# Decay functions and scans of a head, moved between the masks of the head before it

## The chip, the core and the metric

The kernel runs on one core of a Trainium2 chip. The metric is the device time of one execution in microseconds (us); lower is better. The five engines of a core are named as the profile names them: PE (TensorE; PEld is its weight load), DVE (VectorE), ACT (ScalarE), POOL (GpSimd) and SP (SyncE, which issues the DMAs here). Each works through its own instructions in order; they wait for each other by semaphores.

## The reference

One step of a diffusion trunk of two layers for 512 latent and 128 context tokens of width 1024. Layer 0 mixes tokens with HGRN2 (8 heads), layer 1 with GLA (4 heads); each layer ends with a PEER channel mixer, in which most of the time is spent. The change touches the two mixers only. Per head and direction they compute:

```python
# HGRN2: the decay of a head, per direction
f = lb_d + (1.0 - lb_d) * jax.nn.sigmoid(f_pre)
log_f = jnp.log(jnp.maximum(f, F_MIN))
k = (1.0 - lb_d) * jax.nn.sigmoid(-f_pre)
# GLA: the decay of a head, per direction
log_g = jax.nn.log_sigmoid(gk) / GATE_NORM
# both: a chunk of the scan, forward and on reversed tokens
bcum = jnp.cumsum(gi, axis=2)
o_inter = einsum('bhtd,bhde->bhte', qi * jnp.exp(bcum), S)
decay = where(causal, jnp.exp(jnp.minimum(diff, 0.0)), 0.0)
att = einsum('bhtd,bhtsd,bhsd->bhts', qi, decay, ki)
o = o_inter + einsum('bhts,bhse->bhte', att, vi)
S = exp(b_last) * S + einsum('bhsd,bhse->bhde', ki * exp(b_last - bcum), vi)
```

GLA's q, k and v also pass a 3 by 3 depthwise convolution and a silu first.

## The kernel before

`mixer` (line 445) runs both kinds of mixer, one head after the other: `head(h, final)` of each engine stands in a loop over all heads but the last, and once more for the last. Tokens are the 640 columns of every tile, channels the 128 partitions. The order of the work is written out by hand, engine by engine; nothing schedules it.

**Projections.** A head's inputs come from the weight in chunks of 128 columns: HGRN2 has five (v, og, then the early ones ff, fb, q), GLA six (v0, v1, og0, og1, then k, q) and two small gate products. The early chunks of head h + 1 are projected during head h. For each chunk SP loads it (`w_raw`), ACT rounds it (`hi`, line 659, `w_hi`), POOL forms the remainder (`lo`, line 621, `w_lo`), and PE multiplies three times per part (line 440), in two halves of 320 columns with a PSUM bank `pp` each; a half's bank is free for the next chunk once ACT has copied it out (line 679). ACT splits a chunk's weight right behind the copy that frees the buffer (`next_hi`).

**A head, HGRN2.** ACT takes two sigmoids of the gate inputs and one of q (lines 730 to 734). DVE makes the gates of them (856 to 864), ACT takes the logarithm (738), DVE corrects it (870) and scans it, forward and backward, into `b2` (814, 815), which releases POOL by `b_ready`. DVE forms the differences to the chunk's end (876), ACT exponentiates `b2` and them into `e2` and `t2` (742, 743), DVE multiplies q and k in (884, 885) and PE transposes the result and v (975). Then states are formed (984, 901). The seven levels of the in-chunk decay (`exponents`, 556 to 559) are differences, three levels on POOL, four on DVE; ACT exponentiates them (757), DVE weights them with q and k (906, 910) and counts `weighted`. Meanwhile PE projects the early chunks of the next head.

**The mask loop.** For each of five token tiles t, PE computes the scores (996, 997), DVE applies the masks (916, `am`), PE multiplies with v and the states (1013), ACT copies the output (762, `oT`). PE runs the scores of one tile ahead of the products. After the fifth tile the next head begins with its sigmoids on ACT, while PE starts to project its v.

**GLA** differs thus: ACT makes the decay by Abs, Exp and Ln (707 to 711), DVE finishes and scans it (834, 837, 814, 815). In the mask loop DVE has the convolutions of the next head's k and q (794, 803, 805); those of v follow in the head, once v0 and v1 are copied; `silu` (829) and ACT's sigmoid (717) follow each.

POOL's order in a head is: the remainders of chunks 2 and 3, the differences of three levels, the remaining remainders, chunks 0 and 1 of the next head last.

Of the kernel before, what the change touches and what calls it, by code (L numbers as in the profile page):

```python
# [11 lines left out]
ALU = mybir.AluOpType  # L12
ACT = mybir.ActivationFunctionType
# [12 lines left out]
F_MIN = 1e-20  # L26
# [418 lines left out]
def mixer(nc, a, c, mx, h_hi, h_lo, oT, og_sp, out, layer):  # L445
# [15 lines left out]
    with ExitStack() as s:  # L461
# [155 lines left out]
        def _(pool):  # L617
# [6 lines left out]
            def head(h, final):  # L624
                for j in range(2, min(4, NCH)):
                    if j < L or not final:
                        lo(h, j)
                pool.wait_ge(b_ready, h + 1)
                for l in range(POOL_LEVELS):
                    exponents(pool.tensor_tensor, l)  # L630
                    pool.drain().then_inc(pool_diff, 1)
                if not final:
                    for j in range(4, NCH):
                        lo(h, j)
                    lo(h + 1, 0)
                    lo(h + 1, 1)
# [16 lines left out]
        def _(act):  # L653
# [41 lines left out]

            def output_gates(h, n, final):
                if n == 0:
                    act.wait_ge(og_out, h * 16 + 16)
                copy(og[:, n, :], NV + n, h)
                next_hi(h, NV + n, final)  # L700

            def head(h, final):

                if mx.gla:

                    act.drain()
                    act.activation(b2[:, :, :], g2[:, :, :], ACT.Abs)
                    act.drain()
                    act.activation(b2[:, :, :], b2[:, :, :], ACT.Exp, scale=-1.0)
                    act.drain()  # L710
                    act.activation(b2[:, :, :], b2[:, :, :], ACT.Ln, bias=c["one"][:, 0:1])
                    act.drain().then_inc(ln_done, 1)
# [15 lines left out]
                else:  # L728
                    act.drain()
                    act.activation(k2[:, :, :], g2[:, :, :], ACT.Sigmoid, scale=-1.0)  # L730
                    act.drain()
                    act.activation(g2[:, :, :], g2[:, :, :], ACT.Sigmoid)
                    act.drain().then_inc(sig_done, 1)
                    act.activation(zc[:, 1, :], zc[:, 0, :], ACT.Sigmoid).then_inc(q_sig_done, 1)
                    copy(v[:, 0, :], 0, h)
                    next_hi(h, 0, final)
                    act.wait_ge(f_ready, h + 1)
                    act.activation(t2[:, :, :], t2[:, :, :], ACT.Ln).then_inc(ln_done, 1)
# [12 lines left out]
                for n, levels in ((1, (0, 1, 2)), (2, (3, 4, 5, 6)), (3, ())):  # L751
# [6 lines left out]
                    if n < E + mx.extra and not final:  # L758
                        early(h, n)
                for t in range(NT):  # L760
                    act.wait_ge(o_done, h * NT + (1 + t + 1))
                    act.activation(oT[:, bass.ds(h * NV, NV), t * P:(t + 1) * P],
                                   pO[:, 0:NV, :], ACT.Copy).then_inc(o_out, 1)

# [9 lines left out]
            for n in range(E + mx.extra):  # L774
                early(-1, n)
            with act.Fori(0, H - 1) as h:
                head(h, False)
# [3 lines left out]
        def _(dve):  # L781
# [42 lines left out]
            dve.sem_inc(masked, 1)  # L824
            def head(h, final):
                if mx.gla:
                    def silu(j):
# [5 lines left out]
                    dve.wait_ge(ln_done, h + 1)  # L833
                    nc.vector.scalar_tensor_tensor(g2[:, :, :], g2[:, :, :], 0.0, b2[:, :, :],
                                                   ALU.min, ALU.subtract)
                    dve.drain()
                    nc.vector.tensor_scalar(g2[:, :, :], g2[:, :, :], 1.0 / 16.0, None, ALU.mult)
                    dve.drain()
                    scan(h)
# [11 lines left out]
                else:  # L851

                    dve.wait_ge(sig_done, h + 1)
                    for d in range(2):
                        oml = c["oml"][:, bass.ds(h + 8 * d, 1)]
                        nc.vector.tensor_scalar(t2[:, d, :], g2[:, d, :], oml, c["lb"][:, bass.ds(h + 8 * d, 1)],
                                                ALU.mult, ALU.add)
                        nc.vector.tensor_scalar(k2[:, d, :], k2[:, d, :], oml, None, ALU.mult)
                    dve.drain()
                    nc.vector.tensor_scalar(t2[:, :, :], t2[:, :, :], F_MIN, None, ALU.max)  # L860
                    dve.drain()
                    nc.vector.tensor_scalar(g2[:, :, :], t2[:, :, :], LN_LOW, LN_UP, ALU.is_lt, ALU.mult)
                    dve.drain()
                    nc.vector.scalar_tensor_tensor(t2[:, :, :], g2[:, :, :], 1.0, t2[:, :, :], ALU.add, ALU.mult)
                    dve.drain().then_inc(f_ready, 1)
# [3 lines left out]
                    dve.wait_ge(ln_done, h + 1)  # L869
                    nc.vector.scalar_tensor_tensor(g2[:, :, :], g2[:, :, :], LN_FIX, t2[:, :, :], ALU.mult, ALU.add)  # L870
                    dve.drain()
                    scan(h)
# [39 lines left out]
                for t in range(NT):  # L912
# [5 lines left out]
                    if mx.gla and not final and t < 4:  # L918

                        dve.wait_ge(copied, halves_done(h, L + t // 2, 1))  # L920
                        conv(h + 1, t // 2, t % 2)

            if mx.gla:
                for j in range(2):
                    dve.wait_ge(copied, halves_done(-1, L + j, 1))
                    conv(0, j, 0)
                    conv(0, j, 1)
            with dve.Fori(0, H - 1) as h:
                head(h, False)
# [3 lines left out]
        def _(pe):  # L933
# [90 lines left out]
            head(H - 1, True)  # L1024

# [995 lines left out]
```

## Time and profile before

| | |
|---|---|
| median of 3 runs | 5023.19 us (5022.8 to 5024.14) |
| the profiled execution | 5024.39 us, its span 5022.6 us |
| busy, share of the span | PE 84%, PEld 75%, DVE 75%, POOL 38%, ACT 32% |
| a head of HGRN2, from the copies of one to the next | 79.3 us (449.0 to 528.3) |
| a head of GLA | 116.5 us (2887.0 to 3003.5) |

The span is the time from the first instruction's start to the last one's end in the profiled execution; the execution's own time has a little before and after it. Busy shares are means over stages with different limits: the mixers take only part of the span, so what a wait inside a head is worth is read in that head. Times in the rows below are us from the span's start.

### The profile page before, as it was taken

The page shows a single profiled execution, that of the slowest core. Times are in us where ns is not written, and L with a number is a line of the kernel's source. Part 1 is how long each engine was busy: PE and PEld are TensorE (multiplying, and loading weights), DVE is VectorE, ACT ScalarE, POOL GpSimd, SP SyncE. Part 2 cuts the span into 40 slices and gives each one's busy share as a digit, 9 for nine tenths or more (in the row PEclk, how much of TensorE's full clock was granted, in tenths as well). Part 3 has the DMA queues.
Part 4 walks back from the last instruction along what each step waited for, and adds up shares of the span by engine and source line. Part 5 has one row for each costly group of instructions (what it writes and reads, how often), then busy time and mean ns, then how long its engine had stood idle before and what let it go on. Part 6 is the DMA issues. An engine that isn't in the chain of part 4 may idle for free. (4 is left out here: it accounts for less than half of the span.)

```text
span 5022.6 us, 73070 instructions
## 1 busy us (share of the span) xinstructions
PE 4242.4 (84%) x24269; PEld 3745.1 (75%) x24269; DVE 3759.4 (75%) x6839; ACT 1595.5 (32%) x2330; POOL 1893.1 (38%) x1387
## 2 busy tenths in 40 slices
PE   8777877469579999999996778559579999999996
PEld 2177877368469999999995777459468999999995
DVE  0147666629988888899994767637998888899995
ACT  1234333222233333333333333322133333333332
POOL 0023333112245545565661222212144544556662
PEclk9888988689799999999997888779799999999998
DMA  7511110121289999999994111122089999999995
GB/s 256 209 57 42 42 35 29 60 87 48 56 233 371 362 361 362 358 364 362 363 361 144 33 45 35 58 77 66 11 206 365 363 362 361 357 362 365 361 363 217
DMA packets 622019, 1075.57 MB, mean 214 GB/s; under 512 B 230323, under 2 KB 389494, under 8 KB 621174
## 3 DMA queue, kind: packets, MB, share of 16 engines
q1 hardware_dynamic: 473814, 535.07, 31.4%
q0 software_dynamic: 147456, 536.94, 28.8%
q10 hardware_dynamic: 672, 2.62, 0.1%
q8 instruction: 37, 0.61, 0.1%
q14 instruction: 40, 0.33, 0.0%
HBM read 1001.10 MB, written 73.40 MB: 214 GB/s over the span
## 5 line engine op out<-in xcount | busy, mean ns | idle before, releaser
L1710 POOL DMA_INDIRECT rows_ex<-in_peer_v,ctx_index x512 | 707.4, 1382 | 476.2 <-DVE row_acc_ex L1780 360.6
L1710 POOL DMA_INDIRECT rows_ex<-in_peer_u,ctx_index x512 | 586.7, 1146 | 636.8 <-DVE dots_ex L1783 506.0
L1870 PE MATMUL pu_ex<-h_hi,uT_hi_ex 128*128 128x384 f32 x2048 | 715.1, 349 | 1.9 <-ACT coef_ex L1730 1.0
L1780 DVE SCALAR_TENSOR_TENSOR row_acc_ex<-rows_ex,factor_ex,row_acc_ex 128x1024 f32<-128x1024 f32 x512 | 657.7, 1285 | 52.8 <-issue 11.2
L1870 PE MATMUL pu_ex<-h_lo,uT_hi_ex 128*128 128x384 f32 x2048 | 691.9, 338 | 0.0
L1870 PE MATMUL pu_ex<-h_hi,uT_lo_ex 128*128 128x384 f32 x2048 | 691.3, 338 | 0.0
L1878 PE MATMUL py_ex<-v_hi_ex,c_hi_ex 128*128 128x512 f32 x1536 | 622.7, 405 | 0.0
L1783 DVE CUSTOM_DVE_ANT_0 rows_ex<-rows_ex,h_row_ex 128x1024 f32<-128x1024 f32 x512 | 604.5, 1217 | 0.0
L1878 PE MATMUL py_ex<-v_hi_ex,c_lo_ex 128*128 128x512 f32 x1536 | 604.1, 393 | 0.0
L1878 PE MATMUL py_ex<-v_lo_ex,c_hi_ex 128*128 128x512 f32 x1536 | 601.1, 391 | 0.0
L1719 ACT ACTIVATE uT_hi_ex<-pT_ex 128x512 fp32r<-128x512 f32 x512 | 304.5, 595 | 561.3 <-PE pT_ex L1863 507.8
L1771 DVE TENSOR_TENSOR uT_lo_ex<-pT_ex,uT_hi_ex 128x512 fp32r<-128x512 f32 x512 | 351.8, 687 | 167.7 <-ACT uT_hi_ex L1719 159.6
L1725 ACT ACTIVATE v_hi_ex<-v_raw_ex 128x1024 fp32r<-128x1024 f32 x256 | 271.8, 1062 | 486.7 <-PE py_ex L1878 486.7
L1870 PEld LDWEIGHTS pu_ex<-h_hi,uT_hi_ex 128*128 128x128 f32 x2048 | 386.0, 188 | 12.8 <-DVE uT_lo_ex L1771 1.5
L1870 PEld LDWEIGHTS pu_ex<-h_lo,uT_hi_ex 128*128 128x128 f32 x2048 | 386.4, 189 | 9.8
L1870 PEld LDWEIGHTS pu_ex<-h_hi,uT_lo_ex 128*128 128x128 f32 x2048 | 385.1, 188 | 0.0
L621 POOL TENSOR_TENSOR w_lo_hgrn<-w_raw_hgrn,w_hi_hgrn 128x1024 fp32r<-128x1024 f32 x40 | 114.2, 2865 | 615.2 <-ACT w_hi_hgrn L659 612.6
L1878 PEld LDWEIGHTS py_ex<-v_lo_ex,c_hi_ex 128*128 128x128 f32 x1536 | 288.5, 188 | 63.8
L1878 PEld LDWEIGHTS py_ex<-v_hi_ex,c_hi_ex 128*128 128x128 f32 x1536 | 288.9, 188 | 44.5
L1878 PEld LDWEIGHTS py_ex<-v_hi_ex,c_lo_ex 128*128 128x128 f32 x1536 | 289.4, 188 | 43.3
L1794 DVE TENSOR_TENSOR v_lo_ex<-v_raw_ex,v_hi_ex 128x1024 fp32r<-128x1024 f32 x256 | 311.9, 1218 | 0.0
L1863 PE MATMUL pT_ex<-ident,u_raw_ex 128*128 128x128 f32 x2040 | 306.4, 273 | 2.8 <-DVE uT_lo_ex L1771 2.8
(355 smaller groups left out, 8619.5 us busy)
## 6 DMA issues: line engine op xcount, KB each, us to landing
u_raw_ex<-in_peer_u SPq DMA_DIRECT2D x256, 512.0 KB, 6.9
v_raw_ex<-in_peer_v SPq DMA_DIRECT2D x256, 512.0 KB, 6.2
ada<-in_ada_w SPq DMA_DIRECT2D x24, 2048.0 KB, 8.0
gates<-stage_ro SPq DMA_DIRECT2D x12, 4096.0 KB, 15.9
g_raw_ex<-gates SPq DMA_DIRECT2D x256, 192.0 KB, 6.2
w_raw_hgrn<-in_hgrn_w_in SPq DMA_DIRECT2D x40, 512.0 KB, 4.0
w_raw_re<-in_peer_w_q SPq DMA_DIRECT2D x32, 512.0 KB, 4.0
w_raw_gla<-in_gla_w_in SPq DMA_DIRECT2D x25, 512.0 KB, 3.9
```

The lines of the kernel that those rows point to most:

```text
L621: pool.tensor_tensor(w_lo[b][:, :, :], w_raw[b][:, :, :], w_hi[b][:, :, :].bitcast(F32), ALU.subtract).then_inc(w_lo_done, 1)
L1710: pool.indirect_dma_start(out=rows[m % RING][:, :], out_offset=None, in_=a["peer_u" if m < TG * NC else "peer_v"].rearrange("l n d -> (l n ...
L1719: act.activation(uT_hi[b][:, 4 * part:4 * part + 4, :], pT[:, :, :], ACT.Copy) \
L1725: act.activation(v_hi[b][:, :], v_raw[b][:, :], ACT.Copy).then_inc(v_hi_done, 1)
L1771: nc.vector.tensor_sub(uT_lo[b][:, at, :], pT[:, :, :], uT_hi[b][:, at, :].bitcast(F32)) \
L1780: nc.vector.scalar_tensor_tensor(row_acc[g][:, :], rows[j][:, :], factor[:, j:j + 1], row_acc[g][:, :], ALU.mult, ALU.add).then_inc(row_fr ...
L1783: nc.vector.tensor_tensor_reduce(rows[j][:, :], rows[j][:, :], h_row[g][:, :], 1.0, 0.0, ALU.mult, ALU.add, accum_out=dots[:, j:j + 1]).th ...
L1794: nc.vector.tensor_sub(v_lo[b][:, :], v_raw[b][:, :], v_hi[b][:, :].bitcast(F32)).then_inc(v_lo_done, 1)
L1863: last_ = nc.tensor.transpose(pT[:, k, :], u_raw[b][:, (4 * part + k) * P:(4 * part + k + 1) * P], c["ident"][:, :])
L1870: last_ = nc.tensor.matmul(pu[:, 0:TD], w[:, k, :], x[:, k, 0:TD], start=(k == 0 and w is uT_hi[b] and x is h_hi), stop=(k == DC - 1 and w ...
L1878: last_ = nc.tensor.matmul(py[2 * t + i][:, :], w[:, t * P:(t + 1) * P], x[:, i * HALF_D:(i + 1) * HALF_D], start=(first and w is c_hi[b] ...
```

## The change

The decay of a head is computed one head earlier, between the masks and output copies of the preceding head, in pieces. ACT's `decays(h + 1)` stands behind the last early copy of head h and waits for `weighted`, as it overwrites `k2`, which the weighting reads; HGRN2's logarithm (`log_f`) stands behind the third output copy. DVE does a `decay_step` behind each mask from the second on: gates, their lower bound, nothing, and (behind the fifth) the correction and the scans. For GLA only the last step holds anything. The first head's decay is done before the loop. POOL takes the differences of a head before any remainder.

```diff
             def head(h, final):
-                for j in range(2, min(4, NCH)):
-                    if j < L or not final:
-                        lo(h, j)
                 pool.wait_ge(b_ready, h + 1)
                 for l in range(POOL_LEVELS):
                     exponents(pool.tensor_tensor, l)
                     pool.drain().then_inc(pool_diff, 1)
+                for j in range(2, NCH):
+                    if j < L or not final:
+                        lo(h, j)
                 if not final:
-                    for j in range(4, NCH):
-                        lo(h, j)
                     lo(h + 1, 0)
                     lo(h + 1, 1)
...
+            def decays(h, weights_done):
+                act.drain()
+                if weights_done is not None:
+                    act.wait_ge(weighted, weights_done)
                 if mx.gla:
-                    act.drain()
                     act.activation(b2[:, :, :], g2[:, :, :], ACT.Abs)
...
+                else:
+                    act.activation(k2[:, :, :], g2[:, :, :], ACT.Sigmoid, scale=-1.0)
+                    act.drain()
+                    act.activation(g2[:, :, :], g2[:, :, :], ACT.Sigmoid)
+                    act.drain().then_inc(sig_done, 1)
+                    act.activation(zc[:, 1, :], zc[:, 0, :], ACT.Sigmoid).then_inc(q_sig_done, 1)
+            def log_f(h):
+                if not mx.gla:
+                    act.wait_ge(f_ready, h + 1)
+                    act.activation(t2[:, :, :], t2[:, :, :], ACT.Ln).then_inc(ln_done, 1)
...
+                if not final:
+                    decays(h + 1, h + 1)
                 for t in range(NT):
                     act.wait_ge(o_done, h * NT + (1 + t + 1))
                     act.activation(oT[:, bass.ds(h * NV, NV), t * P:(t + 1) * P],
                                    pO[:, 0:NV, :], ACT.Copy).then_inc(o_out, 1)
+                    if t == 2 and not final:
+                        log_f(h + 1)
...
+            decays(0, None)
+            log_f(0)
             with act.Fori(0, H - 1) as h:
...
+                    if not final and t >= 1:
+                        decay_step(h + 1, t - 1)
...
+            for n in range(4):
+                decay_step(0, n)
             with dve.Fori(0, H - 1) as h:
```

`decay_step(h, n)` holds the lines that left DVE's `head`, for HGRN2 lines 856 and 858 in n = 0, 860 to 864 in n = 1, 870 and the scans in n = 3. In the order of the built program, VectorE in the HGRN2 loop, before: the gates stand at the head's start, and the arithmetic of `kdiag` and `q` stands between them and the scans.

```order
L860 TENSOR_SCALAR t_hgrn<-t_hgrn 128x1280
L862 TENSOR_SCALAR g_hgrn<-t_hgrn 128x1280
L864 SCALAR_TENSOR_TENSOR t_hgrn<-g_hgrn,t_hgrn 128x1280
L866 TENSOR_TENSOR kdiag_hgrn<-k_hgrn 128x640
L868 TENSOR_TENSOR q_hgrn<-zc_hgrn 128x640
L870 SCALAR_TENSOR_TENSOR g_hgrn<-g_hgrn,t_hgrn 128x1280
L814 SCALAR_TENSOR_TENSOR b_hgrn<-scan_f,g_hgrn 128x640
L815 SCALAR_TENSOR_TENSOR b_hgrn<-scan_b,g_hgrn 128x640
```

The same instructions in the changed program, from the third mask (line 939, was 916) to the end of the loop's body:

```order
L939 TENSOR_TENSOR am_hgrn<-pA_hgrn,level_mask 128x1024
L861 TENSOR_SCALAR t_hgrn<-t_hgrn 128x1280
L863 TENSOR_SCALAR g_hgrn<-t_hgrn 128x1280
L865 SCALAR_TENSOR_TENSOR t_hgrn<-g_hgrn,t_hgrn 128x1280
L936 REGISTER_ALU
L939 TENSOR_TENSOR am_hgrn<-pA_hgrn,level_mask 128x1024
L936 REGISTER_ALU
L939 TENSOR_TENSOR am_hgrn<-pA_hgrn,level_mask 128x1024
L869 SCALAR_TENSOR_TENSOR g_hgrn<-g_hgrn,t_hgrn 128x1280
L827 SCALAR_TENSOR_TENSOR b_hgrn<-scan_f,g_hgrn 128x640
L828 SCALAR_TENSOR_TENSOR b_hgrn<-scan_b,g_hgrn 128x640
```

The full-tile gate arithmetic now follows the third mask and the scans the fifth; `kdiag` and `q` stay at the head's start. ScalarE at the same place, from the third output copy (line 771, was 762) to the fourth:

```order
L771 ACTIVATE oT<-pO_hgrn 128x128
L716 REGISTER_ALU
L717 ACT_TABLE_LOAD
L717 ACTIVATE t_hgrn<-t_hgrn 128x1280
L770 REGISTER_ALU
L771 ISA
L771 ACTIVATE oT<-pO_hgrn 128x128
```

The logarithm and its table load moved in between the copies. GpSimd at the start of the HGRN2 loop, as a difference:

```order
-L648 ISA
-L621 TENSOR_TENSOR w_lo_hgrn<-w_raw_hgrn,w_hi_hgrn 128x1024
-L619 REGISTER_ALU
-L621 TENSOR_TENSOR w_lo_hgrn<-w_raw_hgrn,w_hi_hgrn 128x1024
-L628 REGISTER_ALU
+L646 UNCONDITIONAL_BRANCH
+L646 ISA
 L556 TENSOR_TENSOR ex_hgrn<-b_hgrn 128x5x64
 L557 TENSOR_TENSOR ex_hgrn<-b_hgrn 128x5x64
```

The two remainders that stood ahead of the differences now stand behind all twelve.

## Rows read from the trace of the kernel before

**Rows 1.** The profile's page, its first line.
```profile
span 5022.6 us, 73070 instructions
```

**Rows 2.** Waits, 449:528.4 us, second HGRN2 head: who waited for whom, us, times, longest.
```profile
DVE t_hgrn L856 <- ACTq L733: 8.3, 1, 8.3
ACT e_hgrn L742 <- DVEq L878: 6.5, 1, 6.5
```

**Rows 3.** Timeline of PE, third HGRN2 head: start us, us, instruction, [idle before <-releaser].
```profile
527.94 0.39 PE L440 MATMUL pp_hgrn<-h_hi,w_hi_hgrn 128*128 128x320 f32 x1
...
559.59 1.76 PE L975 MATMUL pA_hgrn<-ident,t_hgrn 128*128 128x128 f32 x7 [10.10 <-DVEq L886]
```

**Rows 4.** Timeline of ACT, third HGRN2 head.
```profile
551.52 1.27 ACT L742 ACTIVATE e_hgrn<-b_hgrn 128x1280 f32<-128x1280 f32 x1 [6.45 <-DVEq L878]
```

**Rows 5.** Timeline of DVE, second and last HGRN2 head.
```profile
482.45 2.64 DVE L559 TENSOR_TENSOR ex_hgrn<-b_hgrn 128x320 f32<-128x320 f32 x1
...
504.63 0.89 DVE L910 TENSOR_TENSOR ex_hgrn<-ex_hgrn,k_hgrn 128x320 f32<-128x320 f32 x2
...
523.33 1.22 DVE L916 TENSOR_TENSOR am_hgrn<-pA_hgrn,level_mask 128x1024 f32<-128x1024 f32 x1 [2.79 <-PE pA_hgrn L997]
...
854.62 1.49 DVE L864 SCALAR_TENSOR_TENSOR t_hgrn<-g_hgrn,t_hgrn 128x1280 f32<-128x1280 f32 x1
```

**Rows 6.** Timeline of POOL, second and third HGRN2 head.
```profile
504.52 5.53 POOL L621 TENSOR_TENSOR w_lo_hgrn<-w_raw_hgrn,w_hi_hgrn 128x1024 fp32r<-128x1024 f32 x2 [19.77 <-ACT w_hi_hgrn L659]
...
548.79 0.73 POOL L556 TENSOR_TENSOR ex_hgrn<-b_hgrn 128x320 f32<-128x320 f32 x1 [1.46 <-DVEq L817]
549.48 1.30 POOL L557 TENSOR_TENSOR ex_hgrn<-b_hgrn 128x320 f32<-128x320 f32 x1
```

**Rows 7.** Groups of DVE, 449:528.4 us: xcount, busy us, mean ns, idle before.
```profile
L884 DVE TENSOR_TENSOR e_hgrn<-e_hgrn,q_hgrn 128x640 f32<-128x640 f32 x2 | 2.6, 1287 | 0.1
...
L557 DVE TENSOR_TENSOR ex_hgrn<-b_hgrn 128x320 f32<-128x320 f32 x4 | 2.5, 614 | 0.0
...
L558 DVE TENSOR_TENSOR ex_hgrn<-b_hgrn 128x320 f32<-128x320 f32 x4 | 1.9, 484 | 0.0
```

**Rows 8.** Waits, 2887.1:3003.6 us, second GLA head.
```profile
DVE g_gla L834 <- ACTq L712: 14.4, 1, 14.4
...
PE pp_gla L440 <- ACT zc_gla L679: 2.7, 1, 2.7
```

**Rows 9.** Timelines of ACT and DVE, second GLA head.
```profile
2896.70 0.74 ACT L679 ACTIVATE zc_gla<-pp_gla 128x320 f32<-128x320 f32 x2
...
2904.53 0.55 DVE L794 TENSOR_SCALAR v_gla<-zc_gla,vec 128x640 f32<-128x640 f32 x1 [0.30 <-issue]
```

**Rows 10.** Groups of DVE, 2887.1:3003.6 us, second GLA head.
```profile
L805 DVE SCALAR_TENSOR_TENSOR v_gla<-zc_gla,vec,v_gla 128x441 f32<-128x441 f32 (+2 forms) x16 | 17.3, 1083 | 2.0 <-issue 2.0
L805 DVE SCALAR_TENSOR_TENSOR k_gla<-zc_gla,vec,k_gla 128x441 f32<-128x441 f32 (+2 forms) x16 | 11.1, 694 | 2.1 <-issue 2.1
...
L803 DVE SCALAR_TENSOR_TENSOR v_gla<-zc_gla,vec,v_gla 128x127 f32<-128x127 f32 x4 | 3.8, 962 | 0.7 <-issue 0.7
...
L884 DVE TENSOR_TENSOR e_gla<-e_gla,q_gla 128x640 f32<-128x640 f32 x2 | 1.6, 821 | 0.1
...
L803 DVE SCALAR_TENSOR_TENSOR k_gla<-zc_gla,vec,k_gla 128x127 f32<-128x127 f32 x4 | 1.4, 346 | 0.3 <-issue 0.3
...
L837 DVE TENSOR_SCALAR g_gla<-g_gla 128x1280 f32<-128x1280 f32 x1 | 0.8, 826 | 0.1
```

**Rows 11.** Timelines of DVE and PE, first HGRN2 head.
```profile
303.10 1.49 DVE L870 SCALAR_TENSOR_TENSOR g_hgrn<-g_hgrn,t_hgrn 128x1280 f32<-128x1280 f32 x1 [4.00 <-ACT t_hgrn L738]
...
320.09 1.11 PE L975 MATMUL pA_hgrn<-ident,t_hgrn 128*128 128x128 f32 x4 [6.96 <-DVEq L886]
...
345.88 1.41 PE L996 MATMUL pA_hgrn<-ex_hgrn 128*128 128x128 f32 x5 [3.17 <-DVEq L911]
```

**Rows 12.** Timeline of ACT, last HGRN2 head.
```profile
864.98 1.27 ACT L742 ACTIVATE e_hgrn<-b_hgrn 128x1280 f32<-128x1280 f32 x1 [2.83 <-DVEq L878]
```

More of the change, by code:

```diff
@@ L694, in early @@
                 next_hi(h, L + n, False)
+            def decays(h, weights_done):
+                act.drain()
+                if weights_done is not None:
+                    act.wait_ge(weighted, weights_done)
+                if mx.gla:
+                    act.activation(b2[:, :, :], g2[:, :, :], ACT.Abs)
+                    act.drain()
+                    act.activation(b2[:, :, :], b2[:, :, :], ACT.Exp, scale=-1.0)
+                    act.drain()
+                    act.activation(b2[:, :, :], b2[:, :, :], ACT.Ln, bias=c["one"][:, 0:1])
+                    act.drain().then_inc(ln_done, 1)
+                else:
+                    act.activation(k2[:, :, :], g2[:, :, :], ACT.Sigmoid, scale=-1.0)
+                    act.drain()
+                    act.activation(g2[:, :, :], g2[:, :, :], ACT.Sigmoid)
[5 more added lines that the diff above has]
+                    act.activation(t2[:, :, :], t2[:, :, :], ACT.Ln).then_inc(ln_done, 1)
             def output_gates(h, n, final):
@@ L704, in head @@
                 if mx.gla:
-                    act.drain()
[L707 to L712, printed above, removed]
                     convolved = [k2[:, 0, :], k2[:, 1, :], v[:, 0, :], v[:, 1, :]]
@@ L728, in head @@
                 else:
[L729 to L734, printed above, removed]
                     copy(v[:, 0, :], 0, h)
                     next_hi(h, 0, final)
-                    act.wait_ge(f_ready, h + 1)
-                    act.activation(t2[:, :, :], t2[:, :, :], ACT.Ln).then_inc(ln_done, 1)
                     output_gates(h, 0, final)
@@ L824, in _, with decay_step @@
             dve.sem_inc(masked, 1)
+            def decay_step(h, n):
+                if mx.gla:
+                    if n == 3:
+                        dve.wait_ge(ln_done, h + 1)
+                        nc.vector.scalar_tensor_tensor(g2[:, :, :], g2[:, :, :], 0.0, b2[:, :, :],
+                                                       ALU.min, ALU.subtract)
+                        dve.drain()
+                        nc.vector.tensor_scalar(g2[:, :, :], g2[:, :, :], 1.0 / 16.0, None, ALU.mult)
+                        dve.drain()
+                        scan(h)
+                    return
+                if n == 0:
+                    dve.wait_ge(sig_done, h + 1)
+                    for d in range(2):
+                        oml = c["oml"][:, bass.ds(h + 8 * d, 1)]
+                        nc.vector.tensor_scalar(t2[:, d, :], g2[:, d, :], oml, c["lb"][:, bass.ds(h + 8 * d, 1)],
+                                                ALU.mult, ALU.add)
+                        nc.vector.tensor_scalar(k2[:, d, :], k2[:, d, :], oml, None, ALU.mult)
+                    dve.drain()
+                if n == 1:
+                    nc.vector.tensor_scalar(t2[:, :, :], t2[:, :, :], F_MIN, None, ALU.max)
+                    dve.drain()
+                    nc.vector.tensor_scalar(g2[:, :, :], t2[:, :, :], LN_LOW, LN_UP, ALU.is_lt, ALU.mult)
+                    dve.drain()
+                    nc.vector.scalar_tensor_tensor(t2[:, :, :], g2[:, :, :], 1.0, t2[:, :, :], ALU.add, ALU.mult)
+                    dve.drain().then_inc(f_ready, 1)
+                if n == 3:
+                    dve.wait_ge(ln_done, h + 1)
+                    nc.vector.scalar_tensor_tensor(g2[:, :, :], g2[:, :, :], LN_FIX, t2[:, :, :], ALU.mult, ALU.add)
+                    dve.drain()
+                    scan(h)
             def head(h, final):
@@ L831, in silu @@
                         dve.drain()
[L833 to L839, printed above, removed]
                     silu(0)
@@ L851, in head @@
                 else:
[L853 to L865, printed above, removed]
                     nc.vector.tensor_add(kd[:, :], k2[:, 0, :], k2[:, 1, :])
@@ L868, in head @@
                     nc.vector.tensor_mul(q[:, :], zc[:, 0, :], zc[:, 1, :])
[L869 to L872, printed above, removed]
                 for d, e in ((0, P - 1), (1, 0)):
```

## Prediction

> **What bounds the kernel now.** The page's first line gives a span of 5022.6 us [rows 1]. The change touches only the two mixers, eight HGRN2 heads of some 79 us and four GLA heads of some 116 us, so I read the waits inside one head first, then the timelines of the engines in them. In an HGRN2 head VectorE stands 8.3 us until the sigmoids are done, and ScalarE stands 6.5 us at line 742, before the exponentials of the decays, until VectorE has scanned [rows 2]. TensorE starts three projections at 527.94, is through at 549.49 (7.2 us each) and then waits 10.10 us for the products of lines 884 and 885 before it transposes at 559.59 [rows 3]. The reader is to see one chain there: last output copy of a head, sigmoids (ScalarE), gate arithmetic (VectorE), logarithm (ScalarE), scans and differences (VectorE), exponentials (ScalarE), products (VectorE), transposes (TensorE). It runs beside the projections, ends last, and begins only when the preceding head is over. Yet in that head's mask loop VectorE is idle 2.79 us before a mask of 1.22 us [rows 5]. In a GLA head the same place is a wait of VectorE of 14.4 us for Abs, Exp and Ln [rows 8].
>
> **Part 1: sigmoids, gate arithmetic, logarithm and scans move into the mask loop (HGRN2).** Nothing is added: the same instructions issue, and no DMA moves. ScalarE is free between its last weight split and the first output copy; the new wait on `weighted` there has only those output copies queued behind it, and they come later anyway. VectorE's first step, four operations on half tiles, costs at most 4 x 0.82 us (a two-input operation of that size, line 884 in GLA [rows 10]); the second, two scalings of a full tile at 0.83 [rows 10] and line 864 at 1.49 where GpSimd is silent [rows 5], is 3.2 us and some gaps. Either makes the next mask late by 0.6 us at most. Lower bound for that: nothing, as TensorE still has the preceding tile's products to do; upper bound 0.6 us in seven heads, 4 us. I take nothing, because a mask has that slack, and leave the 4 in the range. The logarithm goes between two output copies that are as far apart as the masks, 4 us; a table load and an activation of 1.3 us each (as line 742's own [rows 4]) fit.
>
> So the scans no longer wait for the head to end. The last mask of the example starts at 523.33 and takes 1.22 us [rows 5]; line 870 takes 1.49 us [rows 11], each scan, which runs over half as many columns, as long by my estimate: with gaps 4.6 us, so the scans are done at about 529, where GpSimd's first difference, which waits for them, now starts at 548.79 [rows 6]. What is late next? The exponentials stand in ScalarE's order behind the copies of the second projection, which TensorE ends at 527.94 + 14.4 = 542.3. Then come a weight split and the table load, and the engine is ready at 551.52 - 6.45 = 545.07 [rows 4]. **Gain: the whole 6.45 us wait**, and no more. This is the largest term.
>
> **Part 2: GpSimd takes its differences first.** Twelve of them take 0.73 us each when alone and 1.30 us against VectorE [rows 6], some 9 to 13 us with their gaps. They now run from 529, mostly while VectorE waits, and are over by about 540. So VectorE's four products of lines 884 and 885, 1287 ns on average now [rows 7], cost the clean 821 ns of GLA [rows 10]: 4 x 0.47 = **1.9 us**. Line 557's four calls average 614 ns where line 558's are 484 [rows 7]: **0.5 us**. The price: the remainder of the third weight chunk now stands behind the differences. TensorE wants it at 542.3; done at 540 + 2.4, it is just in time, and a slip of some us is still covered, as the transposes can't start before about 551. The fifth chunk's remainder still meets VectorE's own differences once, as line 559's 2.64 us does now [rows 5].
>
> An HGRN2 head after the first gains 6.45 + 1.9 + 0.5 = 8.9 us; there are six such. The last head has a wait of only 2.83 us at line 742 [rows 12], so 2.8 + 2.4 = 5.2 us.
>
> **The first HGRN2 head pays.** Its decays have no preceding head to hide in, and the remainder waits behind the differences. Line 870 waited 4.00 us for a logarithm that stood behind output copies [rows 11]; that goes, so the scans end at 303.10 - 4.0 + 4.6 = 303.7. Differences against VectorE take 12 us, to 316, the remainder 2.4, then the third projection 7.2 us or, after such a standstill, up to 10: the transposes start near 328 instead of 320.09. From there to the scores the trace has 345.88 - 320.09 = 25.8 us, of which TensorE itself waited 3.17 [rows 11]: 328 + 22.6 = 350.6, a **loss of 4.8 us**. Lower bound 0 (all hidden), upper bound 8. HGRN2 in all: 6 x 8.9 + 5.2 - 4.8 = 53.8 us.
>
> **GLA.** Abs, Exp and Ln leave the head's start. ScalarE's copy of the first projection, at 2896.70 [rows 9], let TensorE wait 2.7 us [rows 8]; its second half was there at about 2894.4. After that half's copy (0.4), a weight split (1.05), a sigmoid (0.7) and a product (0.8) VectorE can start its convolutions at about 2897.7 instead of 2904.53 [rows 9], as the scans are gone from before them: 6.8 us. These two convolutions average 1083 ns for line 805 against 694 ns for the same work in the mask loop, and 962 against 346 ns for line 803 [rows 10]: 16 x 0.389 + 4 x 0.616 = 8.7 us lost to GpSimd. After the change its differences are nearly over before; three remainders still fall into the convolutions, each at most 2.64 - 0.48 = 2.2 us [rows 5, 7], so 8.7 - 6.6 = 2.1 us come back. Gain 8.9 us, in three heads 26.7. The first head pays as in HGRN2: its third chunk's remainder waits 12 us for differences. I take 5 us, between 0 and 10. GLA: 21.7 us.
>
> **Sum.** 53.8 + 21.7 = 75.5 us. The profiled execution took 5024.39 us, 1.8 more than its span; that lies outside the program's instructions and stays. 5024.39 - 75.5 = 4948.9; it stands 1.2 us above the median of the runs shown, so 4947.7, told as **4947 us**.
>
> **A rule against it.** Where both engines meet, the rows show two things. Line 559 at 482.45 was stretched to 2.64 us behind a weight remainder [rows 5]. Yet the two remainders of the next head, asked for at 504.52 in the middle of the weighting, took 5.53 us [rows 6], while line 910 ran on at 0.89 us for two [rows 5], unhindered; so it is in all seven heads that have them. After the change the weighting ends about 9 us earlier, TensorE's projections some 8 us, so these remainders ask 1 to 3 us earlier within the weighting. The Trainium skill, page "SBUF — State Buffer", section "SBUF: two separate sides", says that the port pair of VectorE and GpSimd is an exclusive lock: whichever starts first has it for the whole instruction, and the other fully blocks. By that rule two remainders would hold up the weighting in seven heads, and the sum would be some 46 us, 4977. In line 559 the trace agrees with it, in the weighting not.
>
> **The rivals.** (a) The remainders do get in between the weighting's operations: 2 x 2.2 us in seven heads, 30 us less gain, 4977. For it: line 559 [rows 5]; against: seven of seven weightings. (b) More gain: the first heads cost nothing (9.8 us) and two of three remainders miss the GLA convolutions (4.4 us in three heads): 4947 - 10 - 13 = 4924. For it: TensorE's slack after its projections; against: the differences need some 12 us in a first head. (c) **Slower**: GpSimd's new order starves TensorE in every head. The place is the third projection, whose remainder waits for the scans. It decides once the scans come later than about 531: from then on each us is one of TensorE's, first out of its slack, then out of the head. Were they late in every head, each would pay like the first: 8 x 4.8 + 4 x 5 = 58 us, 5082. It would need the mask loop to delay gate arithmetic or logarithm to the head's end. (d) The change does not do what it says: masks and output copies queue behind the moved steps and stretch the loop by as much as is saved: 5023. Against (c) and (d): the 2.79 us of idle before a mask [rows 5] hold nearly all of each step.
>
> **Chances.** Forecast 0.72 (4935 to 4962 by its own bounds), (a) 0.12, (b) 0.09, (c) 0.04, (d) 0.03. The range reaches from near (b) to (a): 4928 to 4980. A measurement of this kernel can tell 0.2%, 10 us, from no change; so faster 0.93, same 0.03, slower 0.04.
>
> **What would show it.** In the changed profile: nearly no wait of ScalarE for VectorE before the exponentials of an HGRN2 head, a period of about 70 us; TensorE waiting 1 to 2 us instead of 10.1 before the transposes; GpSimd's differences starting around the last output copy; in the first heads TensorE waiting some 11 us for a weight remainder; GLA's convolutions at 0.8 to 0.9 us an operation. Wrong would be shown by weighting operations above 2 us, by masks that start over 1 us late, or by TensorE waiting for remainders in later heads.

## The result, and the profile after

The changed kernel takes **4941.95 us** (median of 4 runs, 4941.39 to 4942.39) against 5022.99 us of the kernel before (4 runs beside it): a ratio of 0.9839 (95% interval 0.9822 to 0.9856), 81.0 us less. Forecast were 4947 us.

By stages, from the ends of the heads' last masks (VectorE's timelines of the two kernels, us):

| stretch | before | after | gain | forecast |
|---|---|---|---|---|
| start to the first HGRN2 head's last mask | 364.62 | 363.86 | 0.76 | -4.8 |
| the next six HGRN2 heads, each | 79.66 | 70.37 | 9.29 | 8.9 |
| the last HGRN2 head | 71.84 | 65.95 | 5.89 | 5.2 |
| from there to the first GLA head's last mask | 1965.80 | 1969.64 | -3.84 | -5 |
| the next three GLA heads, together | 338.01 | 313.07 | 24.94 | 26.7 |
| from there to the end | 1804.37 | 1805.27 | -0.90 | 0 |

In the first row 1.1 us are gained before the first head starts (its first projection starts at 288.31 instead of 289.40), so that head itself loses 0.3 us. No run shows what set that start: in the traces of the other versions it lies between 286.11 and 288.98.

The profile's page, its first line:

```profile
span 4940.0 us, 73082 instructions
```

ScalarE at the exponentials of the third HGRN2 head, the place of [rows 4] (start us, us, instruction, [idle before <-releaser]):

```profile
524.77 1.28 ACT L749 ACT_TABLE_LOAD   x1 [0.16 <-issue]
526.06 1.27 ACT L749 ACTIVATE e_hgrn<-b_hgrn 128x1280 f32<-128x1280 f32 x1
```

The wait of 6.45 us is gone. From the last mask of the head before (it ends at 524.55 [rows 5] and at 505.56 now) to this instruction it was 26.97 us and is 20.50: 6.47 us less. The wait that took its place is VectorE's: 13.27 us until these exponentials, which stand behind ScalarE's copies. VectorE and GpSimd of the same head:

```profile
528.55 0.24 DVE L904 COPY ebl_hgrn<-e_hgrn 128x5 f32<-128x5 f32 x2 [13.27 <-ACTq L751]
528.87 0.83 DVE L907 TENSOR_TENSOR e_hgrn<-e_hgrn,q_hgrn 128x640 f32<-128x640 f32 x1
```

```profile
510.07 0.73 POOL L556 TENSOR_TENSOR ex_hgrn<-b_hgrn 128x320 f32<-128x320 f32 x1 [20.34 <-DVEq L830]
```

The differences start 0.8 us after the start of the last output copy (509.23), and the products take 0.83 us instead of the 1.29 of [rows 7]. TensorE, against [rows 3]:

```profile
531.99 1.31 PE L1002 MATMUL pA_hgrn<-ident,t_hgrn 128*128 128x128 f32 x10 [0.95 <-DVEq L909]
...
556.58 0.76 PE L1023 MATMUL pA_hgrn<-ex_hgrn 128*128 128x128 f32 x2 [5.37 <-DVEq L934]
```

It waits 0.95 us before the transposes instead of 10.10, but 5.37 us before the scores, where it was 3.11. The same scores in the kernel before:

```profile
585.06 1.20 PE L996 MATMUL pA_hgrn<-ex_hgrn 128*128 128x128 f32 x4 [3.11 <-DVEq L911]
```

The scores wait for VectorE's weighting, and from the exponentials on VectorE works without a pause: 33.5 us to the scores before (551.52 to 585.06), 30.5 now (526.06 to 556.58).

TensorE in the first heads, HGRN2 and GLA:

```profile
317.14 0.63 PE L440 MATMUL pp_hgrn<-h_hi,w_hi_hgrn 128*128 128x320 f32 x1 [11.93 <-POOL w_lo_hgrn L621]
...
2733.92 0.63 PE L440 MATMUL pp_gla<-h_hi,w_hi_gla 128*128 128x320 f32 x1 [11.69 <-POOL w_lo_gla L621]
```

VectorE in the second GLA head, groups (xcount | busy us, mean ns), against [rows 10]:

```profile
L818 DVE SCALAR_TENSOR_TENSOR v_gla<-zc_gla,vec,v_gla 128x441 f32<-128x441 f32 (+2 forms) x16 | 15.2, 949 | 2.0 <-issue 2.0
...
L816 DVE SCALAR_TENSOR_TENSOR v_gla<-zc_gla,vec,v_gla 128x127 f32<-128x127 f32 x4 | 3.3, 826 | 0.7 <-issue 0.7
```

1083 ns became 949, and 962 became 826.

### The profile page after: what moved, and what is told of

Its sections match the earlier page's. It is cut to its first block and busy times, and to the rows that moved or that the text cites. A ratio compares the mean times of both kernels' runs of the same rounds, so it can differ in the third digit from the quotient of the medians.

```text
span 4940.0 us, 73082 instructions
## 1 busy us (share of the span) xinstructions
PE 4219.2 (85%) x24269; PEld 3724.8 (75%) x24269; DVE 3704.4 (75%) x6839; ACT 1594.5 (32%) x2328; POOL 1877.7 (38%) x1387
## 5 line engine op out<-in xcount | busy, mean ns | idle before, releaser
L1891 PEld LDWEIGHTS pT_ex<-ident,u_raw_ex 128*128 128x128 f32 x2040 | 253.3, 140 | 49.1 <-issue 3.6
```

Source lines behind the costliest of these rows:

```text
L1891: last_ = nc.tensor.transpose(pT[:, k, :], u_raw[b][:, (4 * part + k) * P:(4 * part + k + 1) * P], c["ident"][:, :])
```

## The experiments

Each ran beside the kernel before on the same chip (its medians there: 5022.4 to 5024.2 us).

**1 and 2: each half of the change alone.** In e1_old_order only GpSimd's order is that of the kernel before; e2_order_alone is the kernel before with GpSimd's new order.

```diff
 # e1: the changed kernel; e2: the kernel before, with the opposite edit
+                for j in range(2, min(4, NCH)):
+                    if j < L or not final:
+                        lo(h, j)
                 pool.wait_ge(b_ready, h + 1)
                 for l in range(POOL_LEVELS):
                     exponents(pool.tensor_tensor, l)
                     pool.drain().then_inc(pool_diff, 1)
-                for j in range(2, NCH):
-                    if j < L or not final:
-                        lo(h, j)
                 if not final:
+                    for j in range(4, NCH):
+                        lo(h, j)
```

> The decays run a head earlier as in the change; GpSimd keeps the order of the kernel before (remainders of chunks 2 and 3 ahead of the differences). Theory on record: the order is a part of its own, worth 2.4 us in each of seven HGRN2 heads (products 1.9, line 557 0.5) and 6.6 us in each of three GLA heads (convolutions), and it costs the first heads the 0.3 and 3.9 us that the changed kernel's trace shows. So 4942 + 16.8 + 19.8 - 4.2 = 4974 us; the products of the HGRN2 heads back at about 1.2 to 1.3 us each, GLA's convolutions of v back near 1.0 us an operation. Rival 1: the order is worth nothing, the early scans alone give the gain: 4938 us. Rival 2: early scans are worth nothing without the order, as the differences start no earlier than the second remainder allows: 5015 us or more.

> The kernel before with GpSimd's new order alone: differences ahead of all remainders, decays where they were. Theory (the slower rival of the prediction, made real): the differences cannot start before the scans, 548.8 in the third head, so they end near 560 and the third projection's remainder near 563 instead of being ready at 542; TensorE waits some 20 us for it in every head, transposes near 571 instead of 559.6. Part of that is absorbed by the wait before the scores (4 to 5 us) and by cleaner products (1.9 us): 3 to 5 us a head are left over in HGRN2, about as much in GLA, so 5050 us (5030 to 5090). Rival: the order works by itself and brings its 2.4 us per HGRN2 head and 6.6 per GLA head: 4985 us.

Measured: e1 4978.34 us (ratio 0.9911, 0.9897 to 0.9924), e2 5064.62 us (1.0084, 1.0070 to 1.0098). The spans of the four kernels:

| | remainders first | differences first |
|---|---|---|
| decays in their own head | 5022.6 | 5064.0 |
| decays a head earlier | 4977.0 | 4940.0 |

**The two halves don't add.** The order alone loses 41 us, and gains 37 once the decays are early. In e2 the remainder waits for late scans, TensorE for the remainder (waits of PE, second loop head, 449.8:531.9: us, times, longest):

```profile
PE pp_hgrn L440 <- POOL w_lo_hgrn L621: 17.2, 1, 17.2
```

That is the mechanism of the prediction's slower rival (c), with its 5082 us too dear: a later HGRN2 head takes 82.0 us instead of 79.7, 2.3 more where (c) had 4.8, and a later GLA head 6.2 more where it had 5. In e1 the exponentials come as early as in the changed kernel, but then GpSimd's differences run into VectorE's products (ScalarE, VectorE and GpSimd, second loop head):

```profile
457.68 1.27 ACT L751 ACTIVATE e_hgrn<-b_hgrn 128x1280 f32<-128x1280 f32 x1
```

```profile
460.94 1.18 DVE L909 TENSOR_TENSOR e_hgrn<-e_hgrn,q_hgrn 128x640 f32<-128x640 f32 x1
462.05 1.35 DVE L910 TENSOR_TENSOR t_hgrn<-t_hgrn,k_hgrn 128x640 f32<-128x640 f32 x1
```

```profile
458.65 0.74 POOL L556 TENSOR_TENSOR ex_hgrn<-b_hgrn 128x320 f32<-128x320 f32 x1
```

The last mask there ends at 437.16, so the exponentials start 20.52 us behind it (20.50 in the changed kernel): ScalarE's 6.45 us are gained in full. But from there to the scores it is 35.2 us (492.92 - 457.68), 1.7 more than before, since the differences start 1 us behind the exponentials' start instead of 2.7 us ahead of it (548.79 and 551.52 [rows 4, 6]). So a head takes 75.2 us, 4.4 less than before on the mean, and the order is worth 4.9 on top, not 2.4. In e1's expectation a term is misread: it gives the order 6.6 us per GLA head, where the prediction has 2.1 come back; by the traces the order is worth 11 us in three GLA heads and 30.6 in the HGRN2 heads behind the first, where the expectation had 19.8 and 16.8; it costs 2.4 us in the first GLA head and nothing in the first HGRN2 head (75.6 us from its first projection to its last mask in both kernels), where it had 3.9 and 0.3. That its 4974 us came close is partly luck.

**3: what caps the gain.** The prediction let the exponentials stand behind the output-gate copies, "and no more" be gained.

```diff
                     next_hi(h, 0, final)
-                    output_gates(h, 0, final)
-                    act.drain().then_inc(og_done, 1)
                 act.wait_ge(e_ready, h + 1)
...
                 act.drain().then_inc(exp_done, 1)
+                if not mx.gla:
+                    output_gates(h, 0, final)
+                    act.drain().then_inc(og_done, 1)
```

> The changed kernel, but in HGRN2 ScalarE takes the exponentials of the decays ahead of the output-gate copies instead of behind them. Theory: what caps the gain of the change is ScalarE's order (VectorE stands 13.3 us until these exponentials, though their inputs are ready at about 444 in the second loop head). With the cap gone VectorE's products, differences and weighting start some 4 to 7 us earlier, and the 5.4 us that TensorE waits before the scores go down to about 0.6: 5 us in each of six heads, about 4 to 6 in the last, nothing in the first (its third projection waits for the remainder): 4907 us. Rival: the weighting is held by the exponentials of levels 3 to 6, which stand behind ScalarE's copies of the early projections, so the scores start no earlier: 4938 to 4942 us.

Measured: 4910.58 us (0.9775, 0.9762 to 0.9789), 31 us less than the changed kernel. The execution that was traced is the slowest of the five, at 4916.92 us; in it the exponentials start 7.2 us earlier in the head (443.46, last mask at 430.13), yet a head gains only 3.3 us (67.1 instead of 70.4 on average): the weight remainders now fall into VectorE's work three times instead of once, and each time cost about 2 us. VectorE, second loop head:

```profile
445.94 2.34 DVE L905 COPY ebl_hgrn<-e_hgrn 128x5 f32<-128x5 f32 x2 [6.08 <-ACTq L749]
...
449.84 3.03 DVE L908 TENSOR_TENSOR e_hgrn<-e_hgrn,q_hgrn 128x640 f32<-128x640 f32 x1
...
457.36 2.47 DVE L556 TENSOR_TENSOR ex_hgrn<-b_hgrn 128x320 f32<-128x320 f32 x1
```

So ScalarE's order was the cap, and behind it comes the share of VectorE's time that GpSimd takes: of the 7.2 us, the two more operations that are stretched take back some 4.2.

**4: the first heads.**

```diff
-            def head(h, final):
+            def head(h, final, first=False):
+                if first:
+                    for j in range(2, 4):
+                        lo(h, j)
...
-                for j in range(2, NCH):
+                for j in range(4 if first else 2, NCH):
...
-            with pool.Fori(0, H - 1) as h:
+            head(0, False, first=True)
+            with pool.Fori(1, H - 1) as h:
```

> The changed kernel, but in the first head of each mixer GpSimd takes the remainders of chunks 2 and 3 ahead of the differences. Theory: the 11.9 us (HGRN2) and 11.7 us (GLA) that TensorE waits for a remainder there go, but only what reaches the mask loop counts: by the two traces 0.3 us in HGRN2 and 3.9 us in GLA, so 4938 us. Rival 1: the first heads pay what was forecast, 4.8 and 5 us: 4932 us. Rival 2: VectorE's convolutions bound the first GLA head, and they collide with the later differences instead: 4942 us, no difference.

Measured: 4937.68 us (0.9832, 0.9818 to 0.9845). By the traces the first HGRN2 head gains 0.9 us, of which 0.4 are left at the end of the eight, and the first GLA head 3.7: the price in HGRN2 is under 1 us, not the 4.8 us of the prediction.

**5: remainders against the weighting.** This tests rival (a) and the rule beside it.

```diff
                         nc.vector.tensor_mul(ks, ks, kv_)
+                    dve.drain()
                 dve.drain().then_inc(weighted, 1)
```

> The changed kernel with VectorE drained after each of the seven levels of the weighting. In the changed kernel the next head's two remainders are asked for at 481.60, in the middle of the second head's weighting, and take 8.13 us, while the weighting runs on at 0.82 and 0.89 us (rival (a) of the prediction would have them get in). Theory 1: a remainder gets in wherever VectorE's queue is empty for a moment; the drains give it such moments, so one or two remainders now stretch the weighting by 2.2 us each in the seven heads that have them: 4942 + 15 to 31, and a few us for the drains: 4960 to 4978 us. Theory 2: what keeps the remainder out is something else (the operands or shapes of the weighting); only the drains cost, under 0.1 us each: 4945 us, no weighting operation above 1 us.

Measured: 4983.38 us (0.9919, 0.9904 to 0.9934), 41 us more than the changed kernel: theory 1, 5 us beyond its upper end. First the changed kernel, GpSimd and VectorE; then this one:

```profile
481.60 8.13 POOL L621 TENSOR_TENSOR w_lo_hgrn<-w_raw_hgrn,w_hi_hgrn 128x1024 fp32r<-128x1024 f32 x2 [17.58 <-ACT w_hi_hgrn L657]
```

```profile
481.23 0.89 DVE L933 TENSOR_TENSOR ex_hgrn<-ex_hgrn,k_hgrn 128x320 f32<-128x320 f32 x2
482.03 0.82 DVE L929 TENSOR_TENSOR ex_hgrn<-ex_hgrn,q_hgrn 128x640 f32<-128x640 f32 x1
```

```profile
489.16 5.39 POOL L621 TENSOR_TENSOR w_lo_hgrn<-w_raw_hgrn,w_hi_hgrn 128x1024 fp32r<-128x1024 f32 x2 [17.58 <-ACT w_hi_hgrn L657]
```

```profile
489.73 5.17 DVE L933 TENSOR_TENSOR ex_hgrn<-ex_hgrn,k_hgrn 128x320 f32<-128x320 f32 x2
```

Undrained, the weighting runs on past the remainders' request; drained, both get in at once and the pair of line 933 takes 5.17 us instead of 0.89. An HGRN2 head takes 75.8 us, 5.4 more. The drains have a price of their own, which theory 1 put at a few us: in the last HGRN2 head, where no remainder asks, the weighting takes 11.86 us instead of 10.87; in the loop heads 16.57, so the two remainders cost 4.7 us a head and the seven drains 1.0.

**6: the slack of a mask.**

```diff
                 if n == 1:
-                    nc.vector.tensor_scalar(t2[:, :, :], t2[:, :, :], F_MIN, None, ALU.max)
-                    dve.drain()
-                    nc.vector.tensor_scalar(g2[:, :, :], t2[:, :, :], LN_LOW, LN_UP, ALU.is_lt, ALU.mult)
-                    dve.drain()
+                    for _ in range(3):
+                        nc.vector.tensor_scalar(t2[:, :, :], t2[:, :, :], F_MIN, None, ALU.max)
+                        dve.drain()
+                        nc.vector.tensor_scalar(g2[:, :, :], t2[:, :, :], LN_LOW, LN_UP, ALU.is_lt, ALU.mult)
+                        dve.drain()
```

> The changed kernel with the first two operations of the gate arithmetic that follows the third mask done three times (the same values again): four operations of 0.83 us with their gaps, 3.6 us more in that place. It measures the slack that the prediction took for granted. In the changed kernel the fourth mask of the second head starts at 501.00, 0.7 us after its scores; TensorE uses it only at 504.13, so it could end 1.9 us later. Theory: only what exceeds this slack costs, 3.6 - 1.9 = 1.7 us in each of seven HGRN2 heads, 4942 + 12 = 4954 us. Rival 1: the mask loop has no slack for VectorE: 7 x 3.6 = 25 us, 4967 us. Rival 2: the scans end the chain, and the loss is made up before the scores: 4942 us.

Measured: 4954.62 us (0.9861, 0.9846 to 0.9876). TensorE's products of the fourth tile, which wait in no such way in the changed kernel:

```profile
510.91 2.05 PE L1041 MATMUL pO_hgrn<-am_hgrn,tt_hgrn 128*128 128x128 f32 x16 [1.59 <-DVE am_hgrn L940]
```

TensorE waits 1.59 us for the mask, so a mask has 3.6 - 1.6 = 2.0 us to spare beyond the moved steps, where 1.9 were expected, and the prediction was right to take nothing for them. The sum, 12.7 us for the expected 12, came out partly by luck: by the traces the first head ends 4.6 us later, since its own decay, which stands ahead of the loop, carries the addition too; the next six take 1.4 us more each and the last 0.8.

**7, 8 and 9: better versions, and the drain again.** e7_combined takes the edits of 3 and 4, counts the two exponentials apart, and in GLA takes the first of them ahead of the sigmoids, with two small VectorE operations moved behind the differences to the chunk's end. e8_no_drains is the changed kernel without the drains between VectorE's products and its differences; e9_combined_no_drains does that to e7.

```diff
 # e7, ScalarE (GLA: the first exponential right behind a wait for b_ready)
                     act.activation(e2[:, :, :], b2[:, :, :], ACT.Exp)
+                    act.drain().then_inc(exp_done, 1)
...
 # e7, VectorE
-                dve.wait_ge(exp_done, h + 1)
+                dve.wait_ge(exp_done, h * 2 + 1)
...
                     nc.vector.tensor_mul(e2[:, d, :], e2[:, d, :], q[:, :])
+                dve.wait_ge(exp_done, h * 2 + 2)
...
 # e8 and e9, VectorE
-                    nc.vector.tensor_mul(t2[:, d, :], t2[:, d, :], k2[:, d, :])
-                dve.drain().then_inc(qk_ready, 1)
+                    last = nc.vector.tensor_mul(t2[:, d, :], t2[:, d, :], k2[:, d, :])
+                last.then_inc(qk_ready, 1)
                 for l in range(POOL_LEVELS, NL):
-                    exponents(nc.vector.tensor_tensor, l)
-                    dve.drain().then_inc(dve_diff, 1)
+                    exponents(nc.vector.tensor_tensor, l).then_inc(dve_diff, 1)
```

> The changed kernel with the two edits that paid (exponentials ahead of the output-gate copies in HGRN2, remainders first in the first heads) and two more: the two exponentials of a head are counted apart, so that VectorE multiplies the first while ScalarE takes the second; and in GLA the first of them stands ahead of the head's sigmoids, with VectorE's kdiag and copy behind its difference. The edits that paid: 4942 - 31.4 - 4.3 = 4906 us. Theory: ScalarE's 1.2 us lie on VectorE's chain in every HGRN2 head (8 x 1.2 = 9.6 us), and in GLA 2.5 us a head can be covered (10 us): 4887 us. Rival: in HGRN2 the products now start with the remainder of the third chunk on GpSimd and lose to it what they gain, so that only GLA gains: 4896 us; or neither does: 4906 us.

> The changed kernel without the five drains between VectorE's products and its four levels of differences: the last instruction of each group counts instead. With drains in the weighting the remainders got in, without them they waited for its end. Theory 1: it is the drain that lets a remainder in. In the changed kernel the fifth chunk's remainder is asked for at 461.43, 0.6 us after the drain behind the products, and stretches line 558 to 2.64 us; without drains it waits until the differences end, and the head gains these 2.2 us and five drains of 0.1 to 0.2 us: 7 heads x 2.9 us in HGRN2 (20 us), and about as much for the remainder in GLA's products in three heads (8 us): 4914 us, unless TensorE then waits for the late remainder. Theory 2: the operands or shapes of the weighting kept the remainders out, the drains there did something else: only the drains' own time is gained, 0.7 us a head: 4934 us, and some difference of about 2.6 us is still there in every head.

> The combined kernel with the same five drains taken out. It took 4892.5 us, and three remainders fall into VectorE's products and differences in each HGRN2 head. Theory 1: the two that are asked for early still get in, as they come right behind the drain after the ebl copies, the third does not: 2.2 + 0.7 us in each HGRN2 head, as far as TensorE's wait before the scores (2.2 us) allows: 15 us, and some us in GLA: 4873 us. Theory 2: only the drains' time: 4886 us.

Measured: e7 4892.50 us (0.9737, 0.9724 to 0.9751); e8 4911.80 us (0.9771, 0.9758 to 0.9784); e9 **4876.01 us** (0.9706, 0.9692 to 0.9719), the fastest version here, 66 us under the changed kernel. e7 lies between its theory (4887) and its rival (4896): its products lose about 4.4 us to two remainders in an HGRN2 head. e8 and e9 come within about 3 us of theory 1. But e8 shows that the drain isn't all of it. GpSimd's remainder of the fifth chunk in two successive heads:

```profile
460.55 8.08 POOL L621 TENSOR_TENSOR w_lo_hgrn<-w_raw_hgrn,w_hi_hgrn 128x1024 fp32r<-128x1024 f32 x1 [5.44 <-ACT w_hi_hgrn L657]
...
526.92 2.37 POOL L621 TENSOR_TENSOR w_lo_hgrn<-w_raw_hgrn,w_hi_hgrn 128x1024 fp32r<-128x1024 f32 x1 [5.46 <-ACT w_hi_hgrn L657]
```

With drains it got in in each of the six loop heads behind the first; without them it waited to the end of the differences in three and still got in in the other three. The last four of these heads take 68.4 (it got in) and 64.7 us (it waited) in turn. Theory 1 had the remainder wait in every head and each gain 2.9 us; the gain is 2 us in the one kind and 5.7 in the other, so that its sum came out is partly luck.

## Why the prediction was right

**The largest term** (6.45 us: "and no more") measured 6.47, and experiment 3 confirms the reason given for its cap. **The second** (2.4 us: cleaner products and line 557) measured 3.0, from the exponentials to the scores. Together 9.5 at one head, 9.29 on the mean, 8.9 forecast. Their split, however, holds only in that order. The prediction priced the order by the collisions of the kernel before; experiment 1 shows that early decays alone would have made these collisions worse by 1.7 us a head, and the order alone, experiment 2, loses. The sum was right because both halves were in it. By the spans the gain is 82.6 us where 75.5 were added up; 5.6 of the 7.1 us between them lie in the first HGRN2 head.

**The step that failed** is the first HGRN2 head: 4.8 us forecast, 0.3 measured. The wait was as told (11.93 us for "some 11"), and the transposes started at 326.02 (forecast 328; 1.1 of these 2.0 us are the head's earlier start). What failed is the step from there: the scores were put 22.6 us behind the transposes, and the last mask was to be as late as they. Measured are 20.7 us to the scores, 1.15 us of wait included, and 17.1 us from there to the end of the last mask instead of 18.7. Experiment 4, which changes nothing in this head but GpSimd's order and so takes the wait away, shows the price directly. Its first scores, and those of the changed kernel:

```profile
343.70 3.33 PE L1027 MATMUL pA_hgrn<-ex_hgrn 128*128 128x128 f32 x14 [5.11 <-DVEq L938]
```

```profile
346.72 1.80 PE L1023 MATMUL pA_hgrn<-ex_hgrn 128*128 128x128 f32 x14 [1.15 <-DVEq L934]
```

Without the wait TensorE transposes 9.75 us earlier (316.27), but its scores, which wait for VectorE, come only 3.0 us earlier, and the last mask only 0.9 (362.97 for 363.86). So 6.7 of the 9.75 us are slack: without the wait it is VectorE's chain that ends last ahead of the scores (in the kernel before it works from 315.00 to 345.61 without a wait for TensorE), and the prediction moved the whole stretch with the transposes. Most of the rest is TensorE's clock, which the prediction took as fixed. Windows of the transposes, before and after (us, busy per engine, then the granted clock, DMA share, GB/s), then of these first scores, experiment 4 and the changed kernel:

```profile
320.00:323.70 3.70, 3.46 (x15) 3.06 (x15) 3.46 (x6) 1.13 (x2) 3.10 (x4) 0.50 0.00 0
```

```profile
326.00:328.00 2.00, 1.81 (x17) 1.56 (x15) 0.94 (x3) 1.79 (x3) 0.32 (x1) 1.00 0.00 0
```

```profile
343.70:347.00 3.30, 3.30 (x15) 3.30 (x16) 0.00 (x0) 3.06 (x3) 3.30 (x2) 0.50 0.00 0
```

```profile
346.70:348.50 1.80, 1.78 (x16) 1.80 (x17) 0.00 (x0) 1.73 (x3) 1.44 (x1) 1.00 0.00 0
```

Before, TensorE had waited 6.96 us ahead of the transposes [rows 11] and ran them at 0.50, the lower of its two levels (1.2 GHz); now it comes from a projection and runs them at 1.00 (2.4 GHz), in half the time. The states that follow gain as much (3.78 to 2.05 us). The first scores come behind 1.15 us of wait and take 1.80 us; behind 3.17 us in the kernel before and 5.11 in experiment 4 they took 3.33.

**GLA**: 24.9 us for 26.7. The convolutions start 18.9 us after the preceding head's last mask instead of 24.3 (2840.56 - 2821.66; 2904.53 - 2880.22), 5.4 us earlier and not 6.8, because the product ahead of them took 2.52 us behind a remainder, where the prediction had put 0.8. Their excess over the mask loop's convolutions fell from 8.7 to 6.0 us, 2.7 for the forecast 2.1. The first GLA head lost 3.8 of the 5 us; there the remainder also holds back the output-gate copies (the first starts at 2739.41, after 15.76 us of idling), behind which ScalarE's sigmoids of v stand (the first at 2744.21).

**What was to show it** was there: no wait of ScalarE ahead of the exponentials, a period of 70.4 us (forecast about 70), 0.95 us before the transposes, weighting operations of 0.82 and 0.89 us, no wait for remainders in later heads. GLA's convolutions, at 0.95 us an operation, lie just above the 0.8 to 0.9 that were told.

**The rivals.** (a) did not come: in the changed kernel the remainders waited out the weighting. By the lock rule of the Trainium skill (page "SBUF — State Buffer", section "SBUF: two separate sides") either engine may be the one that waits; the sum went by the trace and was right to, and experiment 5 shows how near (a) was: one drain per level, and the time is 4983 us. The evidence against (a) was thinner than told: the remainders of [rows 6] did not ask in the middle of the weighting but 1.0 us before its end (504.52, 505.51), and in the seven heads at most 3.0 us before it; in the changed kernel it is 3.6. (b) came for the first HGRN2 head alone. (c) is what the order does without the early decays. (d) is refuted by the time itself, and experiment 6 gives the slack.

## What to carry to other kernels

Price two edits that meet on one engine together: here each half's worth depended on the other, from a loss of 41 us to a gain of 37. When a wait is taken away, read in the trace what stands next in that engine's own order; here the cap was right to 0.1 us, and lifting it was the next 31 us. Before VectorE is drained or made to wait in a place where GpSimd has large operations pending, look at what gets in there.

## What the runs showed of the hardware

**A waiting TensorE pays twice.** In experiment 8 the same scores follow a wait of 4.17 us in one head and of 2.00 us in the next (timeline, then windows of their first tile):

```profile
549.71 0.55 PE L1022 MATMUL pA_hgrn<-ex_hgrn 128*128 128x128 f32 x1 [4.17 <-DVEq L933]
615.93 0.46 PE L1022 MATMUL pA_hgrn<-ex_hgrn 128*128 128x128 f32 x2 [2.00 <-DVEq L933]
```

```profile
549.80:553.00 3.20, 3.20 (x16) 3.20 (x17) 0.00 (x0) 2.98 (x3) 3.20 (x2) 0.53 0.00 0
616.00:617.70 1.70, 1.70 (x16) 1.70 (x17) 0.00 (x0) 1.62 (x3) 1.70 (x1) 1.00 0.00 0
```

After the longer wait the granted clock is 0.53 and the fourteen scores take 3.27 us, after the shorter 1.00 and 1.80. The 2.2 us that a remainder costs VectorE so cost the head 3.6 (68.39 - 64.75): 2.17 of longer wait and 1.47 of slower scores. In the loop heads of the changed kernel the transposes gain 1.6 us in the same way (3.46 us before, 1.86 now), and in four of six the states 1.7 (3.74 to 3.78 before, 2.05 now), but there it only lengthens the wait for VectorE before the scores.

**Who waits, VectorE or GpSimd, hung in part on a drain.** In the changed kernel a remainder asked for 0.6 us behind a drain got in within two instructions, one asked for 7 us into an undrained run waited till its end; with drains in that run (experiment 5) it got in there too, and with the drains of the first place taken out (experiment 8) it waited there in three heads of six. The Trainium skill (page "SBUF — State Buffer", section "SBUF: two separate sides") says that whichever engine starts first has the port pair for the whole instruction, and that there are deep queues which would have to be drained to share it. In the trace it was more than one instruction: the remainder of 481.60 was done 5.82 us later, where one alone takes 2.35, and VectorE's operations of 0.82 and 0.89 us ran on in between. What decides between the three heads and the three, no run here shows. The requests there lie at the same phase of VectorE's instruction within 0.02 us (0.31 us behind the start of line 557 where it waited, 0.33 where it got in and, in another head, where it waited).
